# Cached keys turned by VectorE in the projections and loaded turned in the attention

## The chip, the core and the metric

The kernel runs as one program on one core of a Trainium2 chip. The metric is the device time of the program in microseconds (us). The engines in this text are PE (TensorE, matmuls and transposes; PEld is its weight load), DVE (VectorE), ACT (ScalarE), POOL (GpSimd) and SP (SyncE, which only issues DMA transfers here). SBUF is the core's memory of 128 partitions; PSUM, eight banks of 128 x 512 float32, takes what PE computes. DRAM is the large memory behind the 16 DMA engines.

## The reference

One step of a decoder layer over 1024 prompt tokens and 8 samples of 8 new tokens. All arrays are float32. What the change touches is the attention of the samples over their cached keys: each sample has 8 pages of 128 tokens, found through a page table.

```python
def project(xn, w_in):
    z = xn @ w_in
    q, k, v, a = jnp.split(z, [Q_COLS, Q_COLS + K_COLS, Q_COLS + K_COLS + V_COLS], axis=-1)
    ...
def attend(q, k, v, lam):
    pk = cache_k[l][page_table].reshape(dec_batch, past_len, H_DIFF, 2 * QK_HEAD_DIM)
    pv = cache_v[l][page_table].reshape(dec_batch, past_len, H_DIFF, V_HEAD_DIM)
    k_all = jnp.concatenate([pk.astype(k.dtype), k], axis=1)
    v_all = jnp.concatenate([pv.astype(v.dtype), v], axis=1)
    return diff_attn_core(q, k_all, v_all, qpos, kpos, rel_bias, lam)
def diff_attn_core(q, k, v, qpos, kpos, rel_bias, lam):
    s = jnp.einsum('bqhmd,bkhmd->bhmqk', q, k2) * (QK_HEAD_DIM ** -0.5)
    ...
    p = jax.nn.softmax(s, axis=-1)
    a = p[:, :, 0] - lam * p[:, :, 1]
    return jnp.einsum('bhqk,bkhd->bqhd', a, v)
```

Before it stand an RMS norm and the projection by `w_in`, beside it a spatial gate with a layer norm over `v_a`, behind it `w_out`, a convolutional feed-forward network (`w_up`, `w_down`) and two more norms.

## The kernel before, in words

Each engine has a stream of instructions written out by hand. The engines meet only in semaphores, and an engine that waits holds everything behind it in its stream. There is no scheduler.

**Projections** (the loop over `jobs`; L2094 on PE). `w_in` is taken in ten groups of 256 columns: va, va, u, u, k, k, q, q, v, v. A va or v group is nine jobs (row tiles of 128 tokens, the last of 64), a u, k or q group is six (two halves of columns by three chunks of tokens); each k job is followed by a `gate` job, and the first nine q jobs by a `krow` job. Each job fills one of the eight PSUM banks in turn, so job n waits until the output of job n-8 was copied out. ACT copies va, u and krow jobs (`take_job`), DVE the k, gate, q and v jobs. Weights come in halves of 512 KB from SP (`load_w`, L720), which waits for the half two before; ACT rounds a half into `w_hi` (L727), DVE subtracts into `w_lo` (L733), and PE starts a group when both halves of both are there. DVE does this for group g+1 at the first job of group g. At the first job of the third group (the first u group) it also runs `layer_stats` and `center` for all nine row tiles of va (L1506, L1513), with POOL taking a root and two more passes for each tile in between. Once the first k group starts, the gate jobs need these.

**Attention** (the loop over 32 steps; step i is head i // 8). A step has PE compute scores of 128 queries against 1 to 8 blocks of 128 keys (L2149), DVE their minima with the bias added (L1519, L1528), ACT the exponents (L1000), DVE the mix of the two maps (L1543), PE its transposes (`turn`, L2175) and the products with v (`weigh`, L2187). The scores of a step wait for the exponents of the last that used their banks. The samples' work is put between: for each of 16 units (half the pages of a sample) SP loads four pages of cached keys with tokens on the partitions (`load_keys`, L789), PE transposes each page in four 128 x 128 pieces into a bank of a ring of two (`turn_key`, L2210), DVE and ACT by turns copy the bank into `kt` (`take_keys`, L1559 and L990), and PE computes the samples' scores from it (`smp_scores`, L2233). The ring's two banks are shared with `turn` and with the transposes of the outputs (L2201).

**Afterwards** come `w_out` (L2326), norms, and the feed-forward network (L2383, L2448), where the change does nothing.

## Time and profile before

| | |
|---|---|
| median of 3 runs | 1375.17 us (1374.22 to 1375.6) |
| profiled execution, its span | 1374.4 us |
| DVE busy | 703.4 us (51%) |
| ACT busy | 461.7 us (34%) |
| DMA queues q1, q0, q10: share of 16 engines | 24.5%, 1.6%, 0.7% |
| bytes moved | 113.43 MB, mean 83 GB/s |
| granted TensorE clock | full (2.4 GHz level) in all 40 slices |

The profile gives no other time of the profiled execution than its span, which lies 0.8 us under the median of the runs. Part 2 of the page cuts the span into 40 slices of 34 us; DMA there is the mean busy share of the 16 DMA engines in tenths, GB/s what they moved:

```profile
DMA  8202123256673633132020202011111102020117
GB/s 267 63 31 66 31 70 104 76 178 187 197 209 146 221 103 120 54 108 77 16 76 15 76 15 70 22 61 31 61 31 40 52 15 76 15 73 19 47 47 134
```

The projections are slices 2 to 8, with little traffic; the attention is slices 9 to 14, with most of it. A row of a timeline has the start in us, the duration, the engine, the line, the operation, output<-inputs, the count of merged instructions and in brackets the idle time before them with what ended it. In the rows of a group of instructions (output<-inputs, shapes, count) the numbers after the bar are the busy time in us, the mean of one in ns, and the idle time just before them.

### The profile page before, as it was taken

The numbers are of one execution on the slowest core, as the hardware profiler recorded it, in microseconds if no ns is written. First come the engines' busy times: TensorE is split into PE (matmuls) and PEld (weight loads), VectorE is DVE, ScalarE is ACT, GpSimd is POOL, SyncE is SP. The second block draws the span as 40 slices with busy tenths as digits, with TensorE's granted clock in tenths as the row PEclk, the third lists the DMA queues.
The fourth block names the chain that finished last, engine by engine and source line by source line (L and its number), as shares of the span: only waits on it lengthen the run. The fifth ranks groups of instructions, "written<-read, shape, count | busy, mean of one in ns | idle before, by whom it ended". The sixth has DMA issues, their size and how long they took to land.

```text
span 1374.4 us, 22383 instructions
## 1 busy us (share of the span) xinstructions
PE 1351.8 (98%) x8642; PEld 1216.2 (88%) x8642; DVE 703.4 (51%) x1175; ACT 461.7 (34%) x783; POOL 169.7 (12%) x323
## 2 busy tenths in 40 slices
PE   7999999999999999999999999999999999999998
PEld 6999999966667788899898989898989898999986
DVE  6333412166778564554545464646364545364555
ACT  6321012056666643343131313132313232322332
POOL 2254000021212221120000000000000000000003
PEclk9999999999999999999999999999999999999999
DMA  8202123256673633132020202011111102020117
GB/s 267 63 31 66 31 70 104 76 178 187 197 209 146 221 103 120 54 108 77 16 76 15 76 15 70 22 61 31 61 31 40 52 15 76 15 73 19 47 47 134
DMA packets 93658, 113.43 MB, mean 83 GB/s; under 512 B 6477, under 2 KB 65526, under 8 KB 93590
## 3 DMA queue, kind: packets, MB, share of 16 engines
q1 hardware_dynamic: 90457, 105.52, 24.5%
q0 software_dynamic: 992, 3.54, 1.6%
q10 hardware_dynamic: 2140, 3.46, 0.7%
q8 instruction: 44, 0.72, 0.2%
q14 instruction: 25, 0.20, 0.1%
HBM read 97.28 MB, written 14.69 MB: 81 GB/s over the span
## 4 chain that ended last, share of the span: by engine, by line
PE 93%; DVE 2%; issue 1%; ACT 1%; DMA 1%; SPq 1%; POOL 0%; POOLq 0%; DVEq 0%; ACTq 0%
PE PS L2383 38%; PE PS L2094 17%; PE PS L2448 16%; PE PS L2326 7%; PE PS L2187 2%; PE PS L2149 2%; PE PS L2210 2%; PE PS L2463 2%; PE PS L2478 2%; DMA x_in<-in_x_prompt_dram 1%; PE PS L2256 1%; PE PS L2233 1%; PE PS L2079 1%; PE PS L2317 1%; PE PS L2175 1%
## 5 line engine op out<-in xcount | busy, mean ns | idle before, releaser
L2383 PE MATMUL PS<-act_lo,wu_hi 128*128 128x364 f32 (+1 forms) x1056 | 346.5, 328 | 0.0
L2383 PE MATMUL PS<-act_hi,wu_lo 128*128 128x364 f32 (+1 forms) x1056 | 346.1, 328 | 0.0
L2383 PE MATMUL PS<-act_hi,wu_hi 128*128 128x364 f32 (+1 forms) x1056 | 346.0, 328 | 0.0
L2383 PEld LDWEIGHTS PS<-act_hi,wu_hi 128*128 128x128 f32 x1056 | 198.6, 188 | 0.5
L2383 PEld LDWEIGHTS PS<-act_lo,wu_hi 128*128 128x128 f32 x1056 | 198.2, 188 | 0.4
L2383 PEld LDWEIGHTS PS<-act_hi,wu_lo 128*128 128x128 f32 x1056 | 198.4, 188 | 0.0
L1854 DVE TENSOR_TENSOR y_acc<-y_acc,PS 128x512 f32<-128x512 f32 x162 | 111.1, 686 | 116.1 <-PE PS L2448 116.1
L2448 PE MATMUL PS<-wd_hi,g_hi 128*128 128x512 f32 x324 | 130.2, 402 | 0.0
L2448 PE MATMUL PS<-wd_lo,g_hi 128*128 128x512 f32 x324 | 128.0, 395 | 0.0
L2448 PE MATMUL PS<-wd_hi,g_lo 128*128 128x512 f32 x288 | 114.0, 396 | 0.0
L1239 ACT CAST g_hi<-conv 128x1088 fp32r<-128x1088 f32 x21 | 23.1, 1102 | 245.8 <-PE PS L2448 189.7
L1411 POOL COPY stT<-hsw 128x32 f32 (+1 forms) x22 | 12.6, 571 | 696.5 <-DVE conv L1890 654.6
L2094 PE MATMUL PS<-act_hi,w_hi 128*128 128x364 f32 (+1 forms) x288 | 95.8, 333 | 0.0
L1879 DVE SCALAR_TENSOR_TENSOR conv<-h_gate,cwi,conv 128x1023 f32<-128x1023 f32 x22 | 28.3, 1285 | 131.8 <-ACT conv L1227 131.8
L2094 PE MATMUL PS<-act_lo,w_hi 128*128 128x364 f32 (+1 forms) x288 | 94.5, 328 | 0.0
L2094 PE MATMUL PS<-act_hi,w_lo 128*128 128x364 f32 (+1 forms) x288 | 94.4, 328 | 0.0
L2094 PE MATMUL PS<-w_hi,act_hi 128*128 128x256 f32 x288 | 82.0, 285 | 2.2 <-DVE act_lo L1468 1.5
L2094 PE MATMUL PS<-w_hi,act_lo 128*128 128x256 f32 x288 | 80.9, 281 | 0.0
L2094 PE MATMUL PS<-w_lo,act_hi 128*128 128x256 f32 x288 | 80.4, 279 | 0.0
L2448 PEld LDWEIGHTS PS<-wd_hi,g_hi 128*128 128x128 f32 x324 | 60.8, 188 | 21.5 <-DVE y_acc L1854 8.3
L2448 PEld LDWEIGHTS PS<-wd_lo,g_hi 128*128 128x128 f32 x324 | 60.9, 188 | 12.3
L1879 DVE SCALAR_TENSOR_TENSOR conv<-h_up,cwi,conv 128x1023 f32<-128x1023 f32 x21 | 26.9, 1282 | 84.5 <-ACT conv L1227 84.5
(286 smaller groups left out, 2371.4 us busy)
## 6 DMA issues: line engine op xcount, KB each, us to landing
wu_raw<-in_w_up_dram SPq DMA_DIRECT2D x44, 512.0 KB, 3.9
vpage<-in_cache_v_dram SPq DMA_DIRECT2D x64, 256.0 KB, 3.0
kpage<-in_cache_k_dram SPq DMA_DIRECT2D x60, 256.0 KB, 3.0
wd_raw<-in_w_down_dram SPq DMA_DIRECT2D x22, 512.0 KB, 5.3
w_raw<-in_w_in_dram SPq DMA_DIRECT2D x20, 512.0 KB, 4.7
x_in<-in_x_prompt_dram SPq DMA_DIRECT2D x8, 512.0 KB, 7.8
wo_raw<-in_w_out_dram SPq DMA_DIRECT2D x8, 512.0 KB, 6.0
x_res<-in_x_prompt_dram SPq DMA_DIRECT2D x8, 512.0 KB, 4.4
```

The lines of the kernel that those rows point to most:

```text
L1239: nc.scalar.copy(g2_hi[e][:, NS:] if last else g_hi[:, e, NS:], conv[:, 1, :]).then_inc(g_hi_ready, 1)
L1854: nc.vector.tensor_tensor(dst, dst, PS[:, 6 + half, :], ALU.add).then_inc(ybank_free, 1)
L1879: nc.vector.scalar_tensor_tensor(conv[:, half, NS + 1:], h[:, NS:NTOK - 1], w1, conv[:, half, NS + 1:], ALU.mult, ALU.add).then_inc(tap1_r ...
L2094: mm = nc.tensor.matmul(out, lhs, rhs, start=(i == 0), stop=(i == len(pairs) - 1))
L2149: mm = nc.tensor.matmul(score_cols(i, m)[:, c:e], qT[d, h, qs], kT[d, h, NS + c:NS + e], start=True, stop=True)
L2187: mm = nc.tensor.matmul(PS[:, out_bank(i), 0:DV], at_sb[:, i % 2, P * k:P * k + P], v_all[:, k, DV * h:DV * h + DV], start=(k == 0), stop= ...
L2210: mm = nc.tensor.transpose(PS[:, ring_bank("key", n), P * h:P * h + P], kpage[u][:, p, P * h:P * h + P], ident[:])
L2326: mm = nc.tensor.matmul(PS[:, Y_BANK[t % 2] + half, :], a[:, k, wide(TILES[t])], w[:, 512 * half:512 * half + 512], start=(first and j == ...
L2383: mm = nc.tensor.matmul(PS[:, 3 * half + c, 0:kept(c)], a[:, half, k, :], b[:, k, KEPT[c]], start=(j == 0), stop=(j == len(parts) - 1))
L2448: mm = nc.tensor.matmul(PS[:, 6 + half, :], g, w[:, e, 512 * half:512 * half + 512], start=(j == 0), stop=(j == len(parts) - 1))
L2463: nc.tensor.matmul(PS[:, LAST_BANK[t % 4] + half, :], g, w[:, e, 512 * half:512 * half + 512], start=(j == 0), stop=False)
L2478: mm = nc.tensor.matmul(PS[:, LAST_BANK[t % 4] + half, :], g, w[:, 512 * half:512 * half + 512], start=False, stop=(e == 1 and j == len(pa ...
```

## The change

The cached keys are now turned during the projections. 64 pages are handled as 32 pairs; pair n is the pages 2(n % 2) and 2(n % 2) + 1 of unit n // 2. For each pair SP loads the two pages into one of three buffers `k_tok` (from pair 25 on, two), DVE transposes the buffer in place (`turn_pair`), which turns each 32 x 32 block by itself, and ACT stores it to a DRAM tensor `keys_t` with four transfers, one for each 32 partitions (`store_pair`). In `keys_t` a row is one feature of one page and head, with its 128 tokens; a transfer writes a quarter of each row, 128 bytes. In the attention `load_keys` fetches a unit from `keys_t` with the features on the partitions, in rows of 512 bytes, into one of four buffers, three of which take turns, and PE's key transposes and the 64 copies out of PSUM are gone. `PAIR_SETS` puts pairs 0 to 4 with the second group (va), 5 to 9 with the third (u), 10 to 14 with the fourth, and so on to 29 to 31 with the eighth; `PAIR_AT` spreads a set over the jobs of its group, on DVE and on ACT alike. SP issues a set's loads behind the weights of the group after. The page table is loaded at the start, and some semaphores are merged.

```diff
+    k_tok = [at("k_tok0", 2 * ACT_BYTES + 1024, [P, 2, 512]), at("k_tok1", SCRATCH, [P, 2, 512]),
+             at("k_tok2", keep.at, [P, 2, 512])]
+    keys_t = nc.dram_tensor("keys_t", [2 * NB, 32, 4, 4 * H, P], F32)
...
-    kt = lo_place.put("kt", [P, 2, H, 512])
-    kpage1 = lo_place.put("kpage1", [P, 4, 512])
+    kt_a, kt_b, kt_mid = (lo_place.put(n, [P, 4, H, P]) for n in ("kt_a", "kt_b", "kt_mid"))
...
+    kt = [kt_first] + [kt_a, kt_mid, kt_b] * 5
...
+    PAIR_SETS = [range(0, 5), range(5, 10), range(10, 15), range(15, 20), range(20, 25), range(25, 29), range(29, 32)]
+    TOK_OF = [n % 3 if n < 25 else n % 2 for n in range(NPAIR)]
...
+    PAIR_AT = [jobs_of(k + 1)[j * len(jobs_of(k + 1)) // len(pairs)] for k, pairs in enumerate(PAIR_SETS) for j in range(len(pairs))]
...
+        def load_pair(n):
+            b = TOK_OF[n]
+            if tok_uses(n):
+                sp.wait_ge(ktok_stored[b], 64 * tok_uses(n))
...
+            for a in range(2):
+                at_page = page_index(n // 2, 2 * (n % 2) + a)
+                page = sp.value_load(pages[0:1, at_page:at_page + 1], min_val=0, max_val=n_pool - 1)
+                sp.dma_start(k_tok[b][:, a, :], cache_k[0, bass.ds(page, 1)].rearrange("a t h d -> t (a h d)")).then_inc(slot_loaded[b], 16)
...
         for p in range(4, 2 * len(GROUPS)):
             sp.wait_ge(w_lo_ready, p - 1)
             load_w(sp, p)
+            if p % 2 == 1 and p // 2 - 2 < len(PAIR_SETS):
+                for n in PAIR_SETS[p // 2 - 2]:
+                    load_pair(n)
...
         def load_keys(u):
...
+            if u == 1:
+                sp.wait_ge(kt_loaded[0], 64)
+            if u >= 4:
+                sp.wait_ge(sscore_ready, 2 * (u - 3) + 2)
+            for j in range(4):
+                src = bass.AP(keys_t, u * 32 * 16 * H * P + j * P, [[16 * H * P, 32], [4 * P, 4 * H], [1, P]])
+                sp.dma_start(kt[u][32 * j:32 * j + 32].rearrange("a p h t -> a (p h) t"), src).then_inc(kt_loaded[kt_place(u)], 16)
...
+        def store_pair(n):
+            b, u, p0 = TOK_OF[n], n // 2, 2 * (n % 2)
+            act.wait_ge(ktok_turned, n + 1)
+            for i in range(4):
+                dst = bass.AP(keys_t, u * 32 * 16 * H * P + p0 * 4 * H * P + 32 * i, [[16 * H * P, 32], [P, 8 * H], [1, 32]])
+                src = k_tok[b][32 * i:32 * i + 32].rearrange("a p (c t) -> a (p c) t", t=32)
+                act.dma_start(dst, src).then_inc(ktok_stored[b], 16)
...
+        def turn_pair(n):
+            b = TOK_OF[n]
+            dve.wait_ge(slot_loaded[b], 48 + 32 * (tok_uses(n) + 1))
+            keys = k_tok[b][:].rearrange("p a c -> p (a c)")
+            nc.vector.transpose(keys, keys).then_inc(ktok_turned, 1)
...
+            if n in PAIR_AT:
+                turn_pair(PAIR_AT.index(n))
             if kind in ON_ACT:
                 continue
             dve.wait_ge(job_ready, n + 1)
+            if kind == "q" and n == first_of[g] and half == 0:
+                dve.wait_ge(ktok_stored[2], 64 * TOK_OF.count(2))
...
-        def turn_key(n):
-            u, p = n // 4, n % 4
...
-                mm = nc.tensor.transpose(PS[:, ring_bank("key", n), P * h:P * h + P], kpage[u][:, p, P * h:P * h + P], ident[:])
```

The jobs of the va and u groups are copied by ACT, so DVE passes them without a wait; its pairs 5 to 9 come straight behind the layer statistics. First DVE's stream there (`va<-va` is `center`, `w_lo` a weight half, `kT` the copy of a k job). Before:

```order
L1506 BN_STATS scratch<-va 64x6
L1508 BN_AGGR small<-scratch 64x2
L1513 TENSOR_SCALAR va<-va,small 128x512
L1513 TENSOR_SCALAR va<-va,small 64x512
L733 TENSOR_TENSOR w_lo<-w_raw,w_hi 128x1024 x4
L1690 COPY kT<-PS 128x364
```

And now, in the same place (`k_tok_63`, `64`, `65` are the three buffers):

```order
L1550 TENSOR_SCALAR va<-va,small 64x512
L1545 STREAM_TRANSPOSE k_tok_65<-k_tok_65 128x1024
L1545 STREAM_TRANSPOSE k_tok_63<-k_tok_63 128x1024
L1545 STREAM_TRANSPOSE k_tok_64<-k_tok_64 128x1024
L1545 STREAM_TRANSPOSE k_tok_65<-k_tok_65 128x1024
L1545 STREAM_TRANSPOSE k_tok_63<-k_tok_63 128x1024
L747 TENSOR_TENSOR w_lo<-w_raw,w_hi 128x1024 x2
```

Five transposes, each with a wait for its pages, now stand between the last `center` and the weights of the first k group.

Next ACT's stream through the first u group (`uT` is the copy of a u job, `w_hi` a weight half). Before:

```order
L727 CAST w_hi<-w_raw 128x1024 x2
L919 ACTIVATE uT<-PS 128x364 x2
L919 ACTIVATE uT<-PS 128x360
L919 ACTIVATE uT<-PS 128x364 x2
L919 ACTIVATE uT<-PS 128x360
L727 CAST w_hi<-w_raw 128x1024 x2
```

Now:

```order
L741 CAST w_hi<-w_raw 128x1024 x2
L949 ACTIVATE uT<-PS 128x364
L966 DMA keys_t<-k_tok_65 32x32x32 x4
L949 ACTIVATE uT<-PS 128x364
L966 DMA keys_t<-k_tok_63 32x32x32 x4
L949 ACTIVATE uT<-PS 128x360
L966 DMA keys_t<-k_tok_64 32x32x32 x4
```

The stores of pairs 5, 6 and 7 stand between the u jobs, each behind a wait for DVE's transpose of that pair.

Last PE's stream in a step of the attention. Before:

```order
L2149 MATMUL PS<-kT,qT 128x512 x4
L2201 MATMUL PS<-ident,o_nrm 128x128 x4
L2210 MATMUL PS<-ident,kpage_100 128x128 x8
L2233 MATMUL PS<-kt,qp 32x256 x4
L2187 MATMUL PS<-v_all,at_sb 128x128 x6
```

Now:

```order
L2177 MATMUL PS<-kT,qT 128x512 x4
L2229 MATMUL PS<-ident,o_nrm 128x128 x4
L2251 MATMUL PS<-kt_b,qp 32x256 x4
L2215 MATMUL PS<-v_all,at_sb 128x128 x6
```

The eight key transposes of the step are gone; the rest stands as it did.

## Rows read from the trace of the kernel before

**Rows 1.** the page's first part: engine, busy us, share of the span, instructions

```profile
PE 1351.8 (98%) x8642; PEld 1216.2 (88%) x8642; DVE 703.4 (51%) x1175; ACT 461.7 (34%) x783; POOL 169.7 (12%) x323
```

**Rows 2.** the chain of waits, 50 to 260 us, shares by line

```profile
by line: PE PS L2094 94.3%; PE PS L2079 3.9%; PE PS L2072 1.9%
```

**Rows 3.** groups of instructions, 262 to 480 us: the keys' transposes and copies

```profile
L2210 PE MATMUL PS<-ident,kpage 128*128 128x128 f32 x240 | 33.9, 279 | 2.3 <-ACT res L1024 1.4 <-ACT at_sb L1010 0.9
...
L1559 DVE COPY kt<-PS 128x512 f32<-128x512 f32 x32 | 22.0, 686 | 1.2 <-PE PS L2210 1.2
...
L990 ACT COPY kt<-PS 128x512 f32<-128x512 f32 x32 | 18.8, 587 | 26.0 <-PE PS L2210 26.0
...
L2210 PE MATMUL PS<-ident,kpage_first 128*128 128x128 f32 x16 | 2.5, 286 | 0.7 <-ACT at_sb L1010 0.4 <-DVE kt L1559 0.3
```

**Rows 4.** PE's timeline, two steps of the second head

```profile
340.42 0.66 PE L2210 MATMUL PS<-ident,kpage 128*128 128x128 f32 x4 [0.24 <-ACT res L1024]
...
344.17 1.09 PE L2210 MATMUL PS<-ident,kpage 128*128 128x128 f32 x8
345.19 0.64 PE L2233 MATMUL PS<-kt,qp 128*32 128x256 f32 x8
...
347.76 1.56 PE L2149 MATMUL PS<-kT,qT 64*128 64x512 f32 x8 [0.63 <-ACT prob L1000]
```

**Rows 5.** DVE's timeline, end of the layer statistics and weights behind them

```profile
84.71 0.55 DVE L1513 TENSOR_SCALAR va<-va,small 128x512 f32<-128x512 f32 x1 [2.86 <-POOL small L1327]
...
114.29 0.54 DVE L1513 TENSOR_SCALAR va<-va,small 64x512 f32<-64x512 f32 x1 [3.66 <-POOL small L1327]
114.75 2.34 DVE L733 TENSOR_TENSOR w_lo<-w_raw,w_hi 128x1024 fp32r<-128x1024 f32 x2
```

**Rows 6.** ACT's timeline, last va job, first and ninth u job

```profile
75.01 0.38 ACT L913 ACTIVATE va<-PS 64x256 f32<-64x256 f32 x1 [2.44 <-PE PS L2094]
...
78.99 0.47 ACT L919 ACTIVATE uT<-PS 128x364 f32<-128x364 f32 x1 [1.72 <-PE PS L2094]
...
110.81 0.47 ACT L919 ACTIVATE uT<-PS 128x360 f32<-128x360 f32 x1 [3.47 <-PE PS L2094]
```

**Rows 7.** DVE's timeline, copies of k, q and v jobs

```profile
126.72 0.54 DVE L1690 COPY kT<-PS 128x364 f32<-128x364 f32 x1 [0.18 <-PE PS L2094]
...
222.54 0.54 DVE L1688 TENSOR_SCALAR qT<-PS 128x364 f32<-128x364 f32 x1 [3.89 <-PE PS L2094]
...
244.64 0.42 DVE L1711 COPY v_all<-PS 128x256 f32<-128x256 f32 x1 [2.40 <-PE PS L2094]
```

**Rows 8.** timelines of SP and ACT, DMA issues

```profile
183.86 0.38 ACTq L926 DMA_DIRECT2D out_dram<-k_rows  x1
...
235.07 3.68 SPq L789 DMA_DIRECT2D kpage<-in_cache_k_dram  x4
```

**Rows 9.** the page's sixth part: DMA issues, KB each, median us to landing

```profile
vpage<-in_cache_v_dram SPq DMA_DIRECT2D x64, 256.0 KB, 3.0
...
out_dram<-v_all SPq DMA_DIRECT2D x8, 256.0 KB, 2.0
```

**Rows 10.** DMA, 712 to 722 us, one 512 KB load in 512-byte packets: packets, MB, share

```profile
q1 hardware_dynamic: 1040, 0.52, 18.3%
```

**Rows 11.** DMA, 222.75 to 223.3 us, 128 loads of 264 bytes

```profile
q1 hardware_dynamic: 144, 0.03, 31.9%
```

**Rows 12.** DMA, 223.3 to 223.9 us, loads of 4 bytes

```profile
q1 hardware_dynamic: 97, 0.00, 7.7%
```

**Rows 13.** DMA, 1334.4 to 1336.6 us, stores of 512 bytes (47 closing packets)

```profile
q1 hardware_dynamic: 558, 0.26, 42.5%
```

**Rows 14.** DMA, 268 to 283 us, five v stores in 2-KB packets (80 closing)

```profile
q1 hardware_dynamic: 720, 1.31, 23.0%
```

**Rows 15.** DMA, 284 to 302 us, pages of the cache in 2-KB packets (226 small)

```profile
q1 hardware_dynamic: 2077, 3.79, 71.1%
```

**Rows 16.** DMA, 126 to 132 us, both weight halves of a group

```profile
q1 hardware_dynamic: 1056, 1.05, 56.1%
```

More of the change, by code:

```diff
@@ L333, in own_step @@
         eng.wait_ge(step, steps[id(step)])
-    x_loaded = [sem(f"x_loaded{i}") for i in range(3)]
+    slot_loaded = [sem(f"slot_loaded{i}") for i in range(3)]
     gain_loaded = sem("gain_loaded")
@@ L514, in _program @@
     sbias_loaded = sem("sbias_loaded")
-    sbias_zero = sem("sbias_zero")
     sel_loaded = sem("sel_loaded")
-    page_loaded = sem("page_loaded")
-    kp_loaded = [sem(f"kp_loaded{i}") for i in range(2)]
+    ktok_turned = sem("ktok_turned")
+    ktok_stored = [sem(f"ktok_stored{i}") for i in range(3)]
+    kt_loaded = [sem(f"kt_loaded{i}") for i in range(3)]
     vp_loaded = [sem(f"vp_loaded{i}") for i in range(2)]
@@ L523, in _program @@
     qp_ready = sem("qp_ready")
-    kt_ready = [sem(f"kt_ready{i}") for i in range(2)]
     pv_zero = sem("pv_zero")
@@ L617, in _program, with jobs_of, tok_uses, kt_place @@
     ZERO_STEP = [8, 16, 28, 32]
[L620 to L622 removed]
+    NPAIR = NB * NPAGE // 2
+    PAIR_SETS = [range(0, 5), range(5, 10), range(10, 15), range(15, 20), range(20, 25), range(25, 29), range(29, 32)]
+    TOK_OF = [n % 3 if n < 25 else n % 2 for n in range(NPAIR)]
+    def jobs_of(g):
+        return [n for n, job in enumerate(jobs) if job[1] == g]
+    PAIR_AT = [jobs_of(k + 1)[j * len(jobs_of(k + 1)) // len(pairs)] for k, pairs in enumerate(PAIR_SETS) for j in range(len(pairs))]
+    def tok_uses(n):
+        return TOK_OF[:n].count(TOK_OF[n])
+    def kt_place(u):
+        return max(u - 1, 0) % 3
     ring, ring_taken = [], []
@@ L628, in _program @@
             ring_taken.append((ot_taken, (i - 7) // OB + 1))
-        for n in keys_of(i):
-            ring.append(("key", n))
-            ring_taken.append((kt_ready[n % 2], n // 2 + 1))
         if i >= 1:
@@ L806, in _ @@
         sp.wait_ge(w_lo_ready, 2 * len(GROUPS))
+        for b in range(3):
+            sp.wait_ge(ktok_stored[b], 64 * TOK_OF.count(b))
         load_keys(0)
-        sp.wait_ge(job_ready, first_of[len(GROUPS) - 1])
-        load_keys(1)
         v_jobs = [n for n, job in enumerate(jobs) if job[0] == "v"]
@@ L1747, in _ @@
                     out_norm(i - 3)
-            for n in keys_of(i):
-                if n % 2 == 1 and n not in (3, 5):
-                    take_keys(n)
             if i == 0:
@@ L2202, in turn_out @@
             mm.then_inc(ot_ready, 1)
-        def turn_key(n):
-            u, p = n // 4, n % 4
-            if p == 0:
-                pe.wait_ge(kp_loaded[u % 2], 64 * (u // 2 + 1))
-            pe.wait_ge(*ring_free("key", n))
-            for h in range(H):
-                mm = nc.tensor.transpose(PS[:, ring_bank("key", n), P * h:P * h + P], kpage[u][:, p, P * h:P * h + P], ident[:])
-            mm.then_inc(kturn_ready, 1)
         def own_scores():
@@ L2227, in smp_scores @@
             ks = slice(2 * P * (j % 2), 2 * P * (j % 2) + 2 * P)
-            for i in range(2):
-                pe.wait_ge(kt_ready[i], j + 1)
+            pe.wait_ge(kt_loaded[kt_place(u)], 64 * ((u - 1) // 3 + 1 + (kt_place(u) == 0)))
             if b2 == 0 and u >= 2:
```

102 lines of the change are left out of this document (39 added, 63 removed).

## The prediction

> **What bounds the kernel now.** I read the page's first part first: PE is busy 98% of the span [rows 1]. So an edit pays only where it takes work off PE or adds a wait to it. The chain of waits from 50 to 260 us, the projections, is PE alone, 94.3% of it the products of L2094 and no wait in it [rows 2]. There PE is fed by ACT and DVE far ahead of need, and any stall that the change brings is added whole. The attention, 282 to about 457 us, is mixed. The groups there show what the keys cost: transposes on PE and 64 copies of 128x512 out of PSUM, half by DVE at 686 ns, half by ACT at 587 ns [rows 3]. In PE's timeline a block of eight key transposes takes 1.02 us (344.17 to 345.19), and about every other block of heads 1 and 2 has a wait of 0.2 us or more beside it, for a ring bank or for ACT's exponents, as at 340.42 and 347.76 [rows 4].
>
> **What the change takes away.** 256 transposes are 32 blocks of 1.02 us, 32.6 us of PE. That is the ceiling, with the 3.0 us that PE idles before them (2.3 and 0.7, [rows 3]) about 36. Not all comes back. At 347.76 PE had already stood 0.63 us for ACT's exponents [rows 4]: in the wide steps (five blocks and more) the round scores, minima on DVE, exponents on ACT, scores again is as long as PE's own work, and a block of keys lies inside it. Heads 0 to 2 have four such steps each, head 3 about one and a half. Counting the others: head 0, which opens with 28 transposes and waits for their copies, about 6 us; heads 1 and 2 about 4 us each (four narrow steps of 1.02 us plus a little, of which DVE, busy without a gap there and relieved by only 0.69 us a step, lets 3.5 through, and 0.7 us in the last step); head 3 about 6. I take **20 us**; bounds 12 (DVE's relief in the narrow steps alone) and 36.
>
> **What it adds, and where.** The pages move into the projections as 32 pairs. Each: two page loads (SP issues a page in 0.92 us, 3.68 for four [rows 8]; it lands 3.0 us later [rows 9]), one VectorE transpose of 128x1024, four store issues on ACT (0.38 us each at most [rows 8]), and 4,096 pieces of 128 bytes to DRAM. The transpose is not in the trace. The nearest rows are the 0.55 us of a 128x512 pass over SBUF, doubled to 1.1, and the 1.2 us of each of the two 128x1024 subtractions at 114.75 [rows 5]; I take 1.2 (twice that would still be less than the DMA's time per pair below), 38 us of DVE in all, on an engine that is idle most of this stage. The loads of the turned keys cost what the page loads did: 512 KB in both, in pieces of 512 bytes, and fewer SP instructions. They are hidden as those were.
>
> **The price of a 128-byte piece** decides the case, and none is in the trace. From stretches with one kind of transfer, share times 16 engines times length over packets, after taking 7.6 ns for each closing packet: 512-byte loads 28.5 ns [rows 10], 264-byte loads 21.0 ns [rows 11], 4-byte loads 7.6 ns [rows 12], 512-byte stores 28.6 ns [rows 13], 2-KB stores 85 ns [rows 14]. The line through the two store sizes gives 14.4 ns at 128 bytes, that through the two smallest load sizes above 4 bytes 16.9 ns. I take **16 ns**; bounds 7.6 (the 4-byte packet) and 28.6 (a piece costs as much as a 512-byte one). A pair's store is then 4096 x 16 / 16 engines = 4.1 us of all engines (1.9 to 7.3). Its loads are 256 packets of 2 KB at 110 ns [rows 15], 1.75 us; a group's weights are 53.9 us of one engine [rows 16], 3.4 us, 0.7 per pair. Together 6.5 us per pair.
>
> The Trainium skill (DMA: Bandwidth & Descriptors, Specifications) wants at least 512 bytes for line rate, and says that below it the engine reads, modifies and writes. The 264-byte loads, cheaper than 512-byte ones, do not show that; they are loads, and no store under 512 bytes stands in the trace. By that rule a piece would cost the 28.6 ns of a whole 512-byte store or more, and the sum would be that of the first rival below.
>
> **First stall: the layer statistics.** The new order puts pairs 5 to 9 on DVE behind all layer statistics, and on ACT the store of pair 5 behind the first u job. DVE ends the statistics at 114.8 [rows 5], paced by POOL. Pairs 0 to 4 hold the last va job on ACT until 78.0 where it was done at 75.4 [rows 6], because pair 4 waits for the store of pair 1 and the weights are queued on SP behind it; so all is 2.7 us later, 117.5. ACT, blocked since its first u job (78.99 before [rows 6]), can store pair 5 at 118.7 and take the second u job at 120.5. PE has eight banks: the tenth u job needs the second's. It began at 110.8 before [rows 6], so PE stands 9.7 us. Then pair 8 needs pair 5's buffer: store landed 118.9 + 4.1 + 1.3 = 124.3 (1.3 us is what a 0.7 us store needs beyond its data, 2.0 to landing [rows 9]), pages landed 129.5, turned 130.7. Pair 9 follows the store of pair 6: landed 128.6, turned 134.7. Behind its loads on SP stand the weights of the first k group: issued 130.4, landed among stores about 138, cast and subtracted by 141.2. That group began at 122.7 before (its first copy, 126.72 [rows 7], less 4.0). PE is **18.5 us late** there, in which the 9.7 is contained.
>
> **Second: the DMA engines.** From pair 9 on all that remains needs 15 x 6.5 = 98 us to pair 24 and then 7 x 5.85 + 2 x 3.4 + 6 (the k rows, 9 stores of 0.7) = 54 us to pair 31: turned at 134.7 + 98 + 54 = 286. The buffers, two from pair 25 on, allow 5.9 us per pair and do not bind. DVE turns pair 31 ahead of the copy that stood at 222.54 before; PE can be eight banks ahead, so it stops where the fifth v job ended, 244.6 [rows 7]. It goes on at 286.9. **PE is 42 us late** at the end of the projections, in place of the 18.5. Loads of turned keys wait for all stores (292) and are ready before the attention starts.
>
> **Sum.** 42 - 20 = +22 us. The profiled execution has a span of 1374.4 us, 0.8 under the median of 1375.2; 1374.4 + 22 + 0.8 gives **1397 us**.
>
> **Rivals.** (a) A piece costs 22 ns or more, up to the 28.6 of a 512-byte store. For: the store at 512 bytes costs no less than the load, and partial writes are untried. Against: the 264-byte load. At 28.6 a pair is 7.3 + 2.45 = 9.75 us; pair 9 at 141, pair 24 at 287, pair 31 at 363, PE 119 us late, total 1375 + 119 - 20 = **1474**. (b) The other side: pieces near the 4-byte price. At 7.6 ns a pair needs 4.4 us, less than PE's pace (27 us for five), so only the first stall stays, 15 us since stores 5 and 6 land sooner: 15 - 20 = -5, **1370**. It decides from about 12 ns down, where the 42 has shrunk to the 18 to 20 that the attention gives back; with 30 us given back it would be 1360. For: the 4-byte row. Against: both lines give 14 and more. (c) Between, at 12.5 ns, both sides cancel: **1375**. (d) Pieces at 16 ns, but the attention gives back its ceiling of 36 us: 1381, inside the forecast's own range.
>
> **Chances.** Forecast (13 to 22 ns, 1380 to 1425) 0.43; (a) 0.27; (b) 0.22; (c) 0.08. A measurement of this kernel tells a change from none at about 0.2%, 2.7 us. Faster 0.22, same 0.08, slower 0.70. The range for 8 in 10 runs from 1365, which takes in most of (b), to 1474, the far end of (a).
>
> **What would show it.** In the new profile: store pieces at 16 ns (131,072 of them, 131 us of all 16 engines); DMA near 9 tenths from 120 to 290 us; a PE wait of about 10 us near 110 us on ACT's u copies; the k group's first product near 141; waits of PE in the later groups for DVE copies, and DVE's transposes waiting for DMA; attention starting near 324 and some 20 us shorter, with PE waiting longer for exponents in the wide steps. I am wrong if pieces cost under 12 ns, if ACT or DVE does not stand behind pair 5, or if the attention shrinks by much other than 20 us.

## The result and the profile after

The changed kernel takes 1408.15 us (median of 4 runs, 1406.46 to 1411.49) against 1374.76 for the kernel before (4 runs): ratio 1.0243, 95% interval 1.023 to 1.0255. The forecast was 1397 us, slower, with a range of 1365 to 1474. Its main term, 42 us lost in the projections, came out at 41.9. The attention gave back 8.9 us in place of 20, and that is where the 11 us between 1397 and 1408 lie. The 42, as will be seen, was right in size and in part wrong in how it comes about.

The profiled execution has a span of 1407.6 us, 33.2 more than before. Three places split it: the first scores of the attention (278.44 before, 320.38 after) and the first output product (457.28 before, 490.37 after).

| stretch | before, us | after, us | difference |
|---|---|---|---|
| start to the first scores | 278.44 | 320.38 | +41.9 |
| attention | 178.84 | 169.99 | -8.9 |
| the rest | 917.1 | 917.2 | +0.1 |

The page's first part, and from its second part busy tenths, clock and DMA in 40 slices:

```profile
PE 1330.5 (95%) x8386; PEld 1198.8 (85%) x8386; DVE 721.4 (51%) x1175; ACT 444.9 (32%) x751; POOL 168.6 (12%) x323
...
PE   7995698997887999999999999999999999999998
...
PEclk9998899999999999999999999999999999999999
DMA  7747999948979453232111110202020201110116
```

Against [rows 1] PE has 256 instructions and 21 us less. The clock row has the two eights at 106 to 176 us that no slice had before. The DMA row stands at 9 in the four slices from 141 to 282 us.

The same stretches by engine, of the kernel before and then of the one after (stretch, us, busy us of PE, PEld, DVE, ACT, POOL with their instructions, granted clock, DMA share, GB/s):

```profile
0.00:278.44 278.44, 269.64 (x1900) 264.91 (x1900) 92.69 (x147) 60.71 (x104) 50.61 (x79) 1.00 0.28 88
278.44:457.28 178.84, 171.70 (x1724) 118.32 (x1724) 134.20 (x372) 113.40 (x304) 43.53 (x90) 1.00 0.61 187
```

```profile
0.00:320.38 320.38, 279.89 (x1901) 274.03 (x1901) 127.57 (x179) 60.61 (x104) 48.32 (x79) 0.95 0.76 178
320.38:490.37 169.99, 140.05 (x1468) 91.81 (x1468) 117.23 (x340) 96.80 (x272) 44.72 (x90) 0.98 0.80 201
```

In the projections PE does the same instructions in 10.2 us more of busy time, and idles 40.5 us in place of 8.8: 31.7 us more of waiting, and 10.2 of a slower clock. In the attention it is busy 31.7 us less (the transposes that are gone; the forecast's 32.6) and idles 29.9 us in place of 7.1. So the work did leave PE, and 22.8 us of it came back as waiting.

**Where PE lost the 41.9 us.** PE's timeline, all its waits of 0.4 us or more from 55 to 325 us, with some of the products around the first:

```profile
110.72 0.32 PE L2122 MATMUL PS<-act_hi,w_lo 128*128 128x360 f32 x1
121.29 0.67 PE L2122 MATMUL PS<-act_hi,w_hi 128*128 128x364 f32 x1 [10.25 <-ACT uT L949]
121.76 0.50 PE L2122 MATMUL PS<-act_lo,w_hi 128*128 128x364 f32 x1
...
126.62 0.50 PE L2122 MATMUL PS<-act_hi,w_lo 128*128 128x364 f32 x1
...
127.29 0.33 PE L2122 MATMUL PS<-act_hi,w_lo 128*128 128x364 f32 x1
...
144.54 0.67 PE L2122 MATMUL PS<-act_hi,w_hi 128*128 128x364 f32 x1 [8.46 <-DVE w_lo L747]
...
167.37 0.67 PE L2122 MATMUL PS<-act_hi,w_hi 128*128 128x364 f32 x1 [6.64 <-ACT uT L949]
...
176.76 0.43 PE L2122 MATMUL PS<-act_hi,w_hi 128*128 128x364 f32 x1 [2.43 <-DVE kT L1723]
...
223.23 1.09 PE L2100 MATMUL PS<-ident,kT 128*128 128x128 f32 x4 [4.09 <-DVE kT L1723]
```

Five waits, 31.9 us. Behind each (behind the fourth from 178.2 us) the products come every 0.30 us for some microseconds in place of every 0.17: the granted clock is at its lower level of 1.2 GHz (0.50 in the slice 121.3 to 127.0) and goes back to 2.4. I set the first product of each of the 72 jobs against its time before. PE is 0.3 us late up to 106.9 us, 13.4 from 128 us on, 22.0 at the first k group (144.54), 36.4 from 183 on, 41.9 from 229.3 on. After that nothing is added: it works 91 us without a wait, through pair 31, whose transpose ends at 278.3, and through all v jobs.

What holds ACT and DVE, from their timelines (ACT's copies of u jobs and its store issues; DVE's statistics, transposes and copies):

```profile
79.27 0.47 ACT L949 ACTIVATE uT<-PS 128x364 f32<-128x364 f32 x1
117.92 2.73 ACTq L966 DMA_DIRECT2D keys_t<-k_tok  x4
120.77 0.47 ACT L949 ACTIVATE uT<-PS 128x364 f32<-128x364 f32 x1 [41.02 <-DVE k_tok L1545]
...
160.01 6.71 ACTq L966 DMA_DIRECT2D keys_t<-k_tok  x4
166.84 0.47 ACT L949 ACTIVATE uT<-PS 128x364 f32<-128x364 f32 x1 [9.10 <-issue]
```

```profile
116.65 3.48 DVE L1545 STREAM_TRANSPOSE k_tok<-k_tok 128x1024 f32<-128x1024 f32 x3
129.59 1.25 DVE L1545 STREAM_TRANSPOSE k_tok<-k_tok 128x1024 f32<-128x1024 f32 x1 [9.45 <-DMA k_tok<-in_cache_k_dram]
...
142.12 2.36 DVE L747 TENSOR_TENSOR w_lo<-w_raw,w_hi 128x1024 fp32r<-128x1024 f32 x2 [7.99 <-ACT w_hi L741]
...
220.97 1.25 DVE L1545 STREAM_TRANSPOSE k_tok<-k_tok 128x1024 f32<-128x1024 f32 x1 [0.52 <-DMA k_tok<-in_cache_k_dram]
...
277.09 1.25 DVE L1545 STREAM_TRANSPOSE k_tok<-k_tok 128x1024 f32<-128x1024 f32 x1 [8.19 <-DMA k_tok<-in_cache_k_dram]
```

ACT does nothing from 79.7 to 117.9 us, behind pair 5 and the layer statistics, as forecast [rows 5, 6]. At 160 us it is held by its own four issues: 6.71 us, where [rows 8] had 0.38 us for one; over the 32 pairs the four take 2.3 to 7.5 us. At 221 us DVE turns pair 24 in front of the last copies of k, which PE needs for the k rows.

**The price of a piece.** DMA, 119.5 to 121.5 us, where only stores run (queue, packets, MB, share of 16 engines):

```profile
q10 hardware_dynamic: 2200, 0.28, 96.2%
```

0.962 x 16 x 2.0 us / 2200 = 14.0 ns for a piece of 128 bytes, the line through the two store sizes [rows 13, 14] (14.4) and not my 16. From pair 9 (132.9 us) to pair 24 (221.0) it is 88.1 us, 5.9 a pair where I had 6.5.

The buffers bind as well. Each of the 29 loads that reuse a buffer was issued 0.7 to 1.2 us after the store that frees it had landed, and SP stood 83.3 of 146 us for that (SP's waits, 134 to 280 us):

```profile
SPq L792 <- DMA keys_t<-k_tok: 83.3, 20, 8.7
```

In that stretch the share of the DMA engines is 1.01 up to 222 us on average, but over slices of 4 us it goes from 0.53 (204 to 208 us) to 1.26 (212 to 216), so they aren't full all the time. From pair 24 on, with two buffers, seven pairs took 56 us, 8.0 each, at a mean share of 0.93.

**The attention, head by head**: 41.8, 43.0, 43.1 and 42.1 us, where before it was 41.0, 45.9, 45.9 and 46.1. Head 0 gained nothing, since the second unit's keys came late. PE's waits, 320 to 491 us (engine, line, waited for: us, times, longest), of the kernel after:

```profile
PE PS L2177 <- ACT prob L1033: 11.2, 14, 1.0
PE PS L2215 <- DVE o_nrm L1587: 9.8, 18, 1.0
PE PS L2251 <- DMA kt_a<-keys_t: 4.2, 1, 4.2
PE PS L2251 <- ACT s_prob L1071: 2.5, 3, 1.1
PE PS L2203 <- DVE prob L1580: 1.5, 1, 1.5
```

Before, the scores' wait for ACT's exponents came to 2.1 us, and none for `o_nrm` is listed. The 32 blocks of key transposes, 1.02 us each, had stood in these steps.

### The profile page after: what moved, and what is told of

Read it like the earlier page. It is cut to its first block, busy times and chain, and to the rows that moved or that the text cites. A ratio compares the mean times of both kernels' runs of the same rounds, so it can differ in the third digit from the quotient of the medians.

```text
span 1407.6 us, 21946 instructions
## 1 busy us (share of the span) xinstructions
PE 1330.5 (95%) x8386; PEld 1198.8 (85%) x8386; DVE 721.4 (51%) x1175; ACT 444.9 (32%) x751; POOL 168.6 (12%) x323
## 4 chain that ended last, share of the span: by engine, by line
PE 78%; DVE 4%; POOL 4%; ACTq 4%; DMA 3%; issue 3%; ACT 2%; SPq 1%; DVEq 0%; POOLq 0%
PE PS L2399 37%; PE PS L2464 16%; PE PS L2122 9%; PE PS L2342 7%; ACTq L966 4%; PE PS L2215 2%; PE PS L2479 2%; PE PS L2494 2%; POOL small L1399 1%; DMA keys_t<-k_tok 1%; PE PS L2274 1%; DMA k_tok<-in_cache_k_dram 1%; PE PS L2177 1%; POOL va L1378 1%; POOL va L1380 1%
## 5 line engine op out<-in xcount | busy, mean ns | idle before, releaser
L2122 PE MATMUL PS<-act_hi,w_hi 128*128 128x364 f32 (+1 forms) x288 | 99.9, 347 | 27.8 <-ACT uT L949 16.9
L2122 PE MATMUL PS<-act_hi,w_lo 128*128 128x364 f32 (+1 forms) x288 | 97.8, 339 | 0.0
L2122 PE MATMUL PS<-act_lo,w_hi 128*128 128x364 f32 (+1 forms) x288 | 97.7, 339 | 0.0
L2122 PEld LDWEIGHTS PS<-act_hi,w_hi 128*128 128x128 f32 x288 | 57.3, 199 | 28.8 <-ACT uT L949 17.4
L1033 ACT ACTIVATE prob<-PS,small 128x128 f32<-128x128 f32 (+7 forms) x64 | 47.3, 740 | 87.7 <-DVE small L1565 46.3
```

What stands on the lines that cost most here:

```text
L1033: nc.scalar.activation(dst, score_cols(i, m), ACT.Exp, scale=-1.0, bias=nmax[:, i % 4, m:m + 1], accum_out=prob_sum[:, i % 4, m:m + 1]).th ...
L2122: mm = nc.tensor.matmul(out, lhs, rhs, start=(i == 0), stop=(i == len(pairs) - 1))
```

## The experiments

In the numbers below, "late" is how far the last product of the projections is behind the kernel before in the profiled execution, and "attention" is first scores to first output product. A kernel is already up to 1.6 us ahead or 4.6 us late behind its start-up, before the first pair is loaded, and this part varies from execution to execution; the table at the end has that part beside each lateness. Both are of the one profiled execution, which need not be a median one.

**Larger pieces.** Same bytes, same transfers:

```diff
-dst = ... 32 * i, [[16 * H * P, 32], [P, 8 * H], [1, 32]])
-src = k_tok[b][...].rearrange("a p (c t) -> a (p c) t", t=32)
+dst = ... P * i, [[16 * H * P, 32], [4 * P, 8], [1, P]])
+src = k_tok[b][...].rearrange("a p (c t) -> a (p c) t", t=P)
```

> The changed kernel, but each pair is stored in pieces of 512 bytes, 1,024 instead of 4,096, with the same bytes, the same four transfers and the same waits; the turned keys land in wrong places, so the sample's outputs are not the reference's. Theory 1 (the 16 DMA engines set the lateness: a pair costs 4096 x 14 ns / 16 = 3.6 us of all engines for its store): at 28.6 ns a 512-byte piece the store costs 1.8 us, a pair 4.1 instead of 5.9 us, and what the products lose falls from 41.9 to about 20 us; span 1407.6 - 22 = 1386 us, DMA share in 140 to 220 us near 0.7. Theory 2 (the order of the work does: pair 5 behind the layer statistics, copies behind stores and transposes): the price of a piece matters little, the stalls of 10.25 and 8.46 us at 121 and 144 us stay and later ones shrink by a few us; span 1400 to 1407 us.

Measured: 1391.42 us, ratio 1.0109 (1.0092 to 1.0126), span 1389.8, late 22.9, attention 171.5. The first and second waits stay, smaller; the third is down to 0.66 us and the last is gone:

```profile
117.74 0.67 PE L2122 MATMUL PS<-act_hi,w_hi 128*128 128x364 f32 x1 [7.71 <-ACT uT L949]
137.14 0.67 PE L2122 MATMUL PS<-act_hi,w_hi 128*128 128x364 f32 x1 [5.12 <-DVE w_lo L747]
155.25 0.44 PE L2122 MATMUL PS<-act_hi,w_hi 128*128 128x364 f32 x1 [0.66 <-ACT uT L949]
163.24 0.59 PE L2122 MATMUL PS<-act_hi,w_hi 128*128 128x364 f32 x1 [2.84 <-DVE kT L1723]
```

The size of a piece is worth 19 us of the 41.9 (18.0 without the start-up; by the medians 16.7), near theory 1's 22. It does not explain the rest.

**A quarter of the stores.** Each transfer keeps 256 of its 1,024 pieces:

```diff
-dst = ... [[16 * H * P, 32], [P, 8 * H], [1, 32]])
+dst = ... [[16 * H * P, 32], [P, 2 * H], [1, 32]])
```

> The changed kernel, but each of the four transfers of a pair stores only its first quarter (256 pieces of 128 bytes, 1,024 a pair), and the attention loads its keys in the same pattern of 512-byte pieces from the cache, not from the turned keys; so the sample's outputs are not the reference's. All waits stay. Theory 1 (piece price): the store of a pair costs 0.9 us of all engines, a pair 3.3 us, less than PE's pace of 5; only the first stall with its clock loss stays, 13 to 18 us of lateness; span about 1382 us. Theory 2 (order): stalls of about 10 at 121 us and 6 to 8 at 144 us stay with their clock losses, 22 to 25 us; span 1388 to 1392 us. A third theory, that a transfer's issue on ACT costs by its fixed part and not by its pieces, expects ACT's four issues of a pair to stay at 3.7 us and the total near 1405 us.

Measured: 1386.73 us, ratio 1.0084 (1.0065 to 1.0104), span 1382.8, late 15.1. Theory 1 said 13 to 18 us late and 1382. The profiled execution (1384.54) is the fastest of the four; two others took 1388.58 and 1389.28 (spans of 1386.8 and 1387.6, near theory 2's range), so the times decide less than the lateness does. ACT's four issues take 1.81 us at 114.67 in place of 2.73, so the time of an issue goes with the pieces (its own, and those that wait before it; the run doesn't part the two), and the third theory falls. What is left with a quarter of the pieces is near the price of the order: 15 to 16 us.

**The attention's part alone.** Pair loads, transposes and stores are left out:

```diff
-                for n in PAIR_SETS[p // 2 - 2]:
-                    load_pair(n)
...
-                store_pair(PAIR_AT.index(n))
...
-                turn_pair(PAIR_AT.index(n))
...
-                src = bass.AP(keys_t, u * 32 * 16 * H * P + j * P, ...
+                src = bass.AP(cache_k.tensor, u * 32 * 16 * H * P + j * P, ...
```

> The attention's part of the change alone: pair loads, transposes and stores are left out, and the attention loads its keys in the same pattern of 512-byte pieces from the cache, unturned; so the sample's outputs are not the reference's. The projections should be those of the kernel before (attention starts at 278.4 us), so the time shows what the attention gives back without the stall behind the late keys. In the changed kernel it gave 8.8 us, of which head 0 lost 0.8. If heads 1 to 3 are the true gain (2.8, 2.8, 4.0) and head 0's loss is only the 4.2 us wait for the second unit's keys with a slower clock behind it, that stays here: span 1374.4 - 8.8 = 1365.6 us. If the loss in the attention comes from traffic left by the projections, head 0 gains about 4 us here: 1361 us. My prediction's 20 us would be 1354 us.

Measured: 1366.74 us, ratio 0.993 (0.9914 to 0.9947), span 1367.4, projections on time, attention 172.9. My 20 us are refuted: with nothing to delay it, the lighter attention gives back 6 us in the profiled execution, the slowest of the four (1369.08), and some 8 by the median. Head 0 keeps a wait of 4.6 us for the second unit's keys, so that is no after-effect of the projections. Of the other 3 us against the 8.9, 2.8 lie in heads 1 and 2, where the clock falls as they begin, in this kernel and not in the changed one. Two stretches of 4 us of it, 321.1 to 325.1 and 365.1 to 369.1:

```profile
321.10:325.10 4.00, 3.42 (x21) 2.95 (x22) 3.25 (x19) 1.27 (x7) 0.66 (x2) 0.60 1.24 224
...
365.10:369.10 4.00, 3.04 (x19) 2.51 (x20) 3.25 (x18) 1.72 (x7) 1.10 (x2) 0.64 0.57 101
```

Heads 1 and 2 take 44.4 us here and 43.0 and 43.1 in the changed kernel.

**Stores issued by SP.** The store of pair n-2 stands ahead of the load of pair n on SP; ACT issues none:

```diff
-            if n in PAIR_AT:
-                store_pair(PAIR_AT.index(n))        # on ACT
...
+                    if n >= 3:
+                        for m in ((0, 1) if n == 3 else (n - 2,)):
+                            store_pair(m)           # on SP
                     load_pair(n)
```

> The changed kernel with the pairs' stores issued by SP (the store of pair n-2 ahead of the load of pair n) instead of ACT; all data, sizes and transposes as they were. Theory A (ACT, whose queue is blocked up to 6.7 us by each pair's four issues, sets PE's waits for the u copies): the stalls of 10.25 us at 121 and 6.64 us at 167 go, with their clock losses; PE is about 20 us less late, span 1388 us. Theory B (the DMA engines and the layer statistics ahead of pair 5 set it, and ACT's blocked queue is only where the wait shows): PE gets past 121 us without a stall, but the weights of the first k group, behind the loads on SP, come as late as before or later, lateness at the end of the projections 38 to 46 us, span 1404 to 1412 us.

Measured: 1432.16 us, ratio 1.0408 (1.0385 to 1.0431), span 1429.1, late 62.7. It is outside both ranges, on theory B's side. The waits, PE's timeline:

```profile
141.07 0.67 PE L2125 MATMUL PS<-act_hi,w_hi 128*128 128x364 f32 x1 [18.73 <-DVE w_lo L747]
179.06 0.67 PE L2125 MATMUL PS<-act_hi,w_hi 128*128 128x364 f32 x1 [16.59 <-DVE kT L1726]
...
237.49 1.09 PE L2103 MATMUL PS<-ident,kT 128*128 128x128 f32 x4 [14.13 <-DVE kT L1726]
```

The wait at 121 us is gone and comes back doubled at 141, for the weights, because now SP stands for pair 5. Loads that ran beside the stores stand behind their issue: SP spends 3.35 us on the store issued at 121.28 before the load at 125.47. Moving an issue to another engine moves the wait. The Trainium skill (DMA: Bandwidth & Descriptors, Issuing engines are not separate DMA queues) says that all issuers share the same 16 engines, and that several save only the issuing time, "usually small relative to the DMA itself". The first half is in line with this run: from pair 9 (137.0 us) to pair 24 (236.5) a pair took 6.6 us, no less than with ACT's issues. The second doesn't hold here: in the changed kernel four issues took up to 7.5 us, more than the 3.6 us that their pieces need (4096 x 14.0 / 16).

**Pairs 5 to 9 between the statistics.**

```diff
                         if s >= 1:
                             center(s - 1)
+                            if s in [2, 3, 4, 6, 7]:
+                                turn_pair([2, 3, 4, 6, 7].index(s) + 5)
...
-            if n in PAIR_AT:
+            if n in PAIR_AT and PAIR_AT.index(n) not in range(5, 10):
```

> The changed kernel with one thing moved: VectorE turns pairs 5 to 9 between the steps of the layer statistics (behind the steps 2, 3, 4, 6 and 7), in its waits for POOL, instead of behind all of them. If pair 5 behind the statistics is what opens the lateness (my first stall), the 10.25 us stall at 121 us and the 8.46 us stall at 144 us go with the 4 us of clock loss behind them, the DMA engines start pair 10 near 117 us instead of 134, and 22 pairs of 5.9 us end near 247 us, ahead of the 278 us at which pair 31 was turned; what is left are a few waits of copies behind transposes: 5 to 15 us of lateness, span 1371 to 1381 us. If the DMA engines set the end of the projections anyway (32 pairs x 5.9 us + 20 us of weights in 60 to 278 us), lateness stays above 25 us and the span above 1390 us.

Measured: 1382.68 us, ratio 1.0049 (1.0034 to 1.0064), span 1384.2, late 18.5 (2.5 of it from the start-up: a longer wait for the normed rows at 35 us and a fall of the clock behind it, which the profiled execution of the changed kernel does not have). The one move is worth 25 us of the time (1408.15 - 1382.68). Both waits of 121 and 144 us are gone. Left are 3.31 us at 143, 2.1 at 152 and, largest, the k rows at 200:

```profile
199.67 1.08 PE L2102 MATMUL PS<-ident,kT 128*128 128x128 f32 x4 [6.89 <-DVE kT L1725]
```

The lateness is a little above the range of the first theory and well below the second's 25.

**The second unit's keys early.**

```diff
-    kt = [kt_first] + [kt_a, kt_mid, kt_b] * 5
+    kt_second = at("kt_second", V1, [P, 4, H, P])
+    kt = [kt_first, kt_second, kt_mid, kt_b] + [kt_a, kt_mid, kt_b] * 4
...
+            else:
+                sp.wait_ge(sscore_ready, 4)         # before pages of v that go to the same place
...
         load_keys(0)
+        sp.wait_ge(job_ready, first_of[len(GROUPS) - 1])
+        load_keys(1)
```

> The changed kernel with one thing moved: the turned keys of the second unit go to a place that is free from the last group of products on, and are loaded there before the v stores instead of behind the last product. If the 4.16 us wait for them at 333 us and the half-speed clock from 332 to 338 us are what head 0 lost, the attention gets 6 to 8 us shorter, span 1400 to 1402 us. If PE then only waits elsewhere in head 0 (DVE's and ACT's loop), it gains under 2 us: 1406 us.

Measured: 1407.88 us, ratio 1.0224 (1.0207 to 1.0241): no gain over 1408.15 that these four runs (1401.7 to 1408.89) can tell. The profiled execution says why: head 0 is 37.05 us in place of 41.81, the 4.8 us that were looked for, but heads 1 and 2 take 44.25 and 44.29 with a clock of 0.70 and 0.75 in four microseconds of each (360 to 364, 404 to 408), and the start-up was 4.6 us late: PE waits 4.56 us for the normed rows at 37.4, where it was 1.26, and a fall of the clock follows. Inconclusive by its time, clear for head 0.

**Both moves.**

> Both moves together: pairs 5 to 9 turned between the steps of the layer statistics, and the second unit's turned keys loaded early. If the two losses are independent the times add: 1407.6 - 27 - 7 = 1374 us, with a range of 1363 to 1375; under 1374.4 it beats the kernel before, whose projections are not delayed but whose attention is 8.8 to 16 us longer. If the DMA engines bound the projections, 1385 us or more.

Measured (12 runs): 1378.57 us, ratio 1.003 (1.0016 to 1.0043), span 1376.8, late 13.9, attention 166.8. It is just above the range, and still 0.3% slower than before.

**The pairs spread.** Two versions of the table of sets, with both moves. With the sets the change from three buffers to two moves too, from pair 25 to pair 23 in the first and pair 22 in the second:

```diff
-PAIR_SETS: 5, 5, 5, 5, 5, 4, 3 pairs
+PAIR_SETS: 5, 4, 4, 5, 5, 5, 4 pairs     (first)
+PAIR_SETS: 4, 4, 4, 5, 5, 5, 5 pairs     (second)
```

> The kernel with both moves, with the pairs spread by the length of the groups: 5, 4, 4, 5, 5, 5, 4 in place of 5, 5, 5, 5, 5, 4, 3, the four of the second set turned behind steps 1, 2, 4 and 6 of the layer statistics. There, 13.9 us of lateness came in the two groups of k, from copies that stood behind five pairs of 5.9 us in groups of 24 to 29 us. If the rate of pairs against the DMA engines is the cause, 4 pairs (23.5 us) in the second u group end in time, the k groups start without a backlog, and lateness falls to 3 to 8 us: span 1366 to 1371 us, under the kernel before. If the cause is the order on DVE and ACT alone (a transpose that waits for its pages in front of a copy), it stays at 10 us or more: 1373 to 1377 us.

> The same with 4, 4, 4, 5, 5, 5, 5 pairs: one pair less in the first set, one more in the last. By the rate, the first three groups have slack and the two q groups of 26 us carry 29 us each, which PE's eight banks of lead can take once: lateness 3 to 10 us, more of it at the last q copies, span 1366 to 1373 us. If it is below the run with 5, 4, 4, 5, 5, 5, 4, the backlog began in the first group.

Measured: the first 1377.5 us (11 runs), ratio 1.0024 (1.0012 to 1.0035), late 12.7; the second 1383.8 us (6 runs), ratio 1.0062 (1.005 to 1.0074), late 15.3. The first k group is nearly on time, as the first theory expected (0.0 and -0.7 us at 142, where the start-ups had been 1.6 and 1.4 us ahead), but the totals miss the 3 to 8 and 3 to 10 us: the backlog moved, to the k rows and to the last q copies. The second's profiled execution (1379.31 us) is the fastest of its six. In the first version PE's and DVE's timelines show the place:

```profile
189.55 0.66 PE L2106 MATMUL PS<-ident,kT 128*128 128x128 f32 x2 [6.79 <-DVE kT L1729]
```

```profile
183.67 1.25 DVE L1549 STREAM_TRANSPOSE k_tok<-k_tok 128x1024 f32<-128x1024 f32 x1 [4.68 <-DMA k_tok<-in_cache_k_dram]
185.60 0.53 DVE L1729 COPY kT<-PS 128x364 f32<-128x364 f32 x1
187.30 1.25 DVE L1549 STREAM_TRANSPOSE k_tok<-k_tok 128x1024 f32<-128x1024 f32 x1 [1.17 <-DMA k_tok<-in_cache_k_dram]
188.47 0.94 DVE L1729 COPY kT<-PS 128x364 f32<-128x364 f32 x2
```

A transpose that waits for its pages holds the copies behind it.

**One pair less ahead of the last k copy.** 5, 5, 4, 5, 4, 5, 4 pairs, the second set behind steps 1, 2, 4, 5 and 7.

> As the kernel with both moves, with 5, 5, 4, 5, 4, 5, 4 pairs, those of the second set turned behind steps 1, 2, 4, 5 and 7 of the layer statistics. With 5, 4, 4, 5, 5, 5, 4 the stall that was left was one of 6.79 us at 189.6 us: TensorE turns the k rows there and needs the last k copies, which stood on VectorE behind two transposes that waited for pages. If the DMA engines' rate (5.9 us a pair) against the place of that last k copy is the cause, one pair less in front of it and one more in the idle 80 to 90 us take the stall away: 2 to 7 us of lateness with the two q groups, span 1364 to 1370 us, below the kernel before. If the DMA engines' total sets the end, the backlog only moves into the q groups, as with 4, 4, 4, 5, 5, 5, 5: lateness 10 us or more, span 1373 us or more.

Measured (11 runs): 1375.53 us against 1375.61, ratio 0.9996 (0.9985 to 1.0007), the same as before within the measurement; late 12.9 in the profiled execution, which at 1378.73 us is the slowest of the eleven. The 1364 to 1370 was a miss. The wait at the k rows shrank from 6.79 to 3.83 us and others opened (1.80 at 144.5, 1.84 at 252.8). The DMA share is 0.97 to 1.01 in each 30 us from 120 to 240 us. That is the second theory's outcome: a rate sets it, not a place. Whether this rate is that of the DMA engines alone is not shown. Over 4 us their share goes from 0.56 to 1.27 here too, and again each load from pair 3 on follows the landing of the store that frees its buffer by 0.7 to 1.3 us. A round through one of three buffers (load, transpose, issue on ACT behind the pair before, landing) gets shorter with fewer pieces just as the engines' work does. A run with a fourth buffer would part the two; there is none.

**The same with pieces of 512 bytes.**

> The last kernel (5, 5, 4, 5, 4, 5, 4 pairs) with its stores in pieces of 512 bytes, as in the first experiment: the same bytes, the turned keys in wrong places, so the sample's outputs are not the reference's. If the 128-byte pieces on the DMA engines are what still keeps the projections 12.9 us late, they are now on time (0 to 2 us late) and only the attention's gain is left: 1374.4 - 12 = 1362 us, up to 2 us more for a clock that falls at a head's start. If the order on VectorE and ACT keeps them late, lateness stays above 6 us and the span above 1368 us.

Measured: 1364.88 us, ratio 0.9928 (0.9911 to 0.9945), span 1361.0, late -1.1, attention 166.6. The -1.1 us are there behind the start-up already, and nothing is added. So the whole lateness of the best order goes with the 128-byte pieces: 12.3 us without the start-ups. The two profiled executions are the slowest of one kernel and the fastest of the other; the medians are 10.7 us apart. With it gone the change would be worth 10 us, no more.

| kernel | median, us | ratio | late, us | of it start-up, us | attention, us |
|---|---|---|---|---|---|
| changed | 1408.15 | 1.0243 | 41.9 | 0.3 | 170.0 |
| pieces of 512 bytes | 1391.42 | 1.0109 | 22.9 | -0.7 | 171.5 |
| a quarter of the stores | 1386.73 | 1.0084 | 15.1 | -1.3 | 172.2 |
| attention alone | 1366.74 | 0.993 | -1.3 | -1.3 | 172.9 |
| stores by SP | 1432.16 | 1.0408 | 62.7 | -0.4 | 170.3 |
| between the statistics | 1382.68 | 1.0049 | 18.5 | 2.5 | 170.3 |
| second unit early | 1407.88 | 1.0224 | 44.2 | 4.6 | 167.5 |
| both | 1378.57 | 1.003 | 13.9 | 0.1 | 166.8 |
| 5, 4, 4, 5, 5, 5, 4 | 1377.5 | 1.0024 | 12.7 | -1.6 | 166.8 |
| 4, 4, 4, 5, 5, 5, 5 | 1383.8 | 1.0062 | 15.3 | -1.4 | 166.8 |
| 5, 5, 4, 5, 4, 5, 4 | 1375.53 | 0.9996 | 12.9 | 0.6 | 168.5 |
| the same, 512 bytes | 1364.88 | 0.9928 | -1.1 | -1.1 | 166.6 |

## Why the prediction came out as it did

**The attention's 20 us** is the term that was mis-sized: 8.9. By heads I had 6, 4, 4 and 6; measured -0.8, 2.8, 2.8 and 4.0. In head 0 I wrote that loads of turned keys "are ready before the attention starts". That holds for the first unit only. The second goes to a place that is free when the last product is done, and SP issues it at 325.26; PE waits 4.16 us at 333.1 and then works at the lower clock. Loaded early, head 0 is 4 us shorter than before, 37.05 against 41.0. In heads 1 and 2 the wide steps did what I said: 388.23 to 393.39 and 393.39 to 399.05 are 5.16 and 5.66 us, and before they were 5.16 and 5.66 (393.62, 398.78, 404.44, in head 2). But the narrow ones were held too. The stretch of a head up to its first wide step, before and after:

```profile
365.29:393.62 28.33, 27.13 (x331) 19.58 (x330) 17.43 (x59) 15.92 (x49) 5.21 (x15) 1.00 0.54 159
```

```profile
405.22:431.27 26.05, 22.10 (x290) 15.33 (x290) 14.84 (x54) 13.86 (x46) 5.67 (x15) 1.00 0.69 174
```

Five blocks, 5.0 us, left PE, and the stretch is 2.3 us shorter, where I had 3.5. I had taken DVE's load as what limits it, and DVE is busy only 14.8 of 26.0 us; but the long waits fall where it is busy. The chain behind `o_nrm` is: weighted sum on PE, the sum of its squares on ACT (L1049), the factor on POOL (L1401), `o_nrm` on DVE, next weighted sum. At the longest of these waits (POOL's, DVE's and PE's timelines) the factor is there at 423.37:

```profile
423.18 0.19 POOL L1401 TENSOR_TENSOR small<-small 128x1 f32<-128x1 f32 x1
...
424.08 0.62 DVE L1580 SCALAR_TENSOR_TENSOR prob<-prob,small,prob 128x384 f32<-128x384 f32 x1
424.62 0.34 DVE L1587 SCALAR_TENSOR_TENSOR o_nrm<-PS,small,sub_gain 128x128 f32<-128x128 f32 x1
...
425.11 0.57 PE L2215 MATMUL PS<-v_all,at_sb 128*128 128x128 f32 x3 [0.97 <-DVE o_nrm L1587]
```

DVE comes to `o_nrm` 1.25 us later, without a gap behind the minima and the mix of other steps. It is so four times in heads 1 and 2, 3.7 of the 9.8 us: there DVE's order and its work at that moment hold PE. In the other waits for `o_nrm` DVE takes the factor 0.04 us after POOL has it, and the limit is the round trip itself. So the step was right in naming DVE, and wrong in counting on its mean load. I read this from the timelines; no run shortened the chain or moved `o_nrm` on DVE.

**The first stall**, 9.7 us at 110.8 forecast, was 10.25, of the cause named. That it opens the lateness is shown by the run with the pairs between the statistics. The first k group was forecast 18.5 us late at 141.2; it was 22.0 late at 144.54. Missing were mostly 2.7 us of slow clock behind the stall.

**The 42 us at the end.** I had PE stop where the fifth v job's copy stood and go on at 286.9, when pair 31 was turned. There was no such stop. Pair 31 was turned at 278.3, pieces being 14.0 ns and not 16. With my own rule that would have made 35 us (279.2 - 244.6). In its place PE lost 41.9 us earlier, in five waits up to 223 us: the DMA engines were as busy as forecast, but each set of five pairs held copies or weights that the groups needed, so that PE paid in the second u group, in the first k group and at the k rows, and 10 us of the lower clock were in no term. "The buffers ... do not bind" was wrong too: every load stood behind the landing that freed its buffer. Two errors of about 7 us cancelled. So the sum's main term was right by luck in its last digits. That the price of the pieces and the work queued behind them make it is shown by the two runs with 512-byte pieces (without the start-ups 18.0 us less late in the changed order, 12.3 in the best one) and by the move of five transposes; whether the pieces act through the engines' rate, as I had it, or through the round of the three buffers is open.

**The price of a piece.** 14.0 ns where few stores are queued, inside my 7.6 to 28.6 and near the lower of the two lines. The rule of the Trainium skill (DMA: Bandwidth & Descriptors, Specifications) that I had as the first rival's ground, that below 512 bytes an engine reads, modifies and writes, I had read as a small piece costing at least a 512-byte one. It doesn't here: 14.0 ns against 31.9 for 512 bytes into the same tensor, worked out below. The rule's other half, that line rate wants at least 512 bytes, agrees in its direction: 9 bytes a nanosecond against 16; the 2-KB stores of [rows 14] reach 24. Rival (a) is out by this. Rival (b) needed 12 ns or less, and with more stores queued the pieces do go at one each 10.2 ns (below); what puts it out is the 5.9 us a pair in place of its 4.4.

**The issue on ACT.** I took 0.38 us each; four took 2.3 to 7.5 us. It cost nothing of its own that a run shows: moved to SP it was worse. But it is how the full DMA queues reach ACT's copies, at 167 us.

**The transposes** cost 1.2 us each as taken (32, mean 1.235), 39.2 us of DVE. They hold PE where they wait for pages; what their own 1.2 us cost no run shows by itself.

## What to carry to other kernels

Price a stage that is handed to the DMA engines by pieces, then ask of each engine's queue what stands behind the wait: here more than half of the loss was the placing of five transposes behind a slow chain on VectorE, and one move gave back 25 us. Ask of each buffer too when its next load can start. Work taken off the busiest engine comes back only up to the next round trip between the others; count that loop in each kind of step, narrow ones too, with what each engine has in front of its link at that moment. And add the clock: an engine that stood for some microseconds did its next ones at half speed.
